# Expert weights loaded as 2 MiB units in 16 KB pieces, gate before up, with all gathers ahead of gate's second half

## The reference

```
x <- LN1(alpha * x + (sum_b sigmoid(G_b) * (mixer_b @ w_branch[b])) @ w_out)
# hierarchical MoE: softmax over 4 groups, best group; top 2 of its 4 experts
h   = silu(x @ w_gate[e]) * (x @ w_up[e])        # [tokens, 512] per expert, 16 experts
ffn = sum_e combine[t, e] * (h[e] @ w_down[e])   # [tokens, 2048]
x <- LN2(alpha * x + ffn)
```

## Time and profile before

| | |
|---|---|
| median of the runs | 1325.91 us |
| the profiled execution's own time | 1324.61 us |
| its span in the profile | 1322.9 us |
| PE busy | 1308.2 us |
| DMA moved | 364.97 MB, mean 276 GB/s |
| TensorE's granted clock | full speed |

### The profile page before, as it was taken

How to read it: one execution, slowest core, us unless ns; L and a number is a source line. 1 busy time by engine, 2 the same in 40 slices (tenths; PEclk the granted TensorE clock), 3 DMA queues, 4 the chain that set the end, 5 groups by cost and what they waited for, 6 DMA issues and landing times.

```text
span 1322.9 us, 17951 instructions
## 1 busy us (share of the span) xinstructions
PE 1308.2 (99%) x7379; PEld 959.7 (73%) x7379; DVE 569.2 (43%) x741; ACT 476.6 (36%) x667; POOL 29.5 (2%) x55
## 2 busy tenths in 40 slices
PE   9999999999999999999999999999999999999998
PEld 9999989998888888888888888844453444544443
DVE  4367445356555644464455555525112121221206
ACT  4535343346556544454333433422121121211212
POOL 1000000400000000000100001000000000000000
PEclk9999999999999999999999999999999999999999
DMA  9965555544454445554556795699999999999996
GB/s 302 344 230 197 175 190 188 190 160 160 159 161 156 160 154 194 174 174 159 191 190 226 262 393 178 264 416 416 422 420 422 420 421 421 421 421 420 422 408 253
DMA packets 122100, 364.97 MB, mean 276 GB/s; under 512 B 11627, under 2 KB 19243, under 8 KB 98486
## 3 DMA queue, kind: packets, MB, share of 16 engines
q1 hardware_dynamic: 115430, 359.06, 73.1%
q10 hardware_dynamic: 6608, 5.02, 1.3%
HBM read 361.96 MB, written 2.10 MB: 275 GB/s over the span
## 4 chain that ended last, share of the span: by engine, by line
PE 93%; DMA 3%; DVE 2%; ACT 0%; issue 0%; SPq 0%; DVEq 0%; ACTq 0%
PE main L1212 19%; PE main L1214 19%; PE main L1213 19%; PE main L556 16%; PE att L646 7%; PE att L510 5%; DMA mraw<-in_expert_w_down_dram 3%; PE att L1453 1%; PE main L522 1%; PE main L523 1%; PE att L1436 1%; PE att L1472 1%; PE att L1468 1%; DVE wlo L1866 1%; PE att L1423 0%; PE att L617 0%
## 5 line engine op out<-in xcount | busy, mean ns | idle before, releaser
L1866 DVE TENSOR_TENSOR wlo<-raw,whi 128x2048 fp32r<-128x2048 f32 x135 | 310.3, 2299 | 360.3 <-ACT whi L1619 360.3
L1619 ACT ACTIVATE whi<-raw 128x2048 fp32r<-128x2048 f32 x135 | 258.1, 1912 | 420.4 <-PE main L1214 418.9
L556 PE MATMUL main<-mraw,xg 128*64 128x512 f32 x1024 | 225.4, 595 | 1.5 <-DMA mraw<-in_expert_w_up_dram 1.4
L1212 PE MATMUL main<-whi,xhi 128*128 128x512 f32 (+1 forms) x544 | 203.9, 375 | 0.0
L1214 PE MATMUL main<-whi,xlo 128*128 128x512 f32 (+1 forms) x544 | 201.7, 371 | 0.0
L1213 PE MATMUL main<-wlo,xhi 128*128 128x512 f32 (+1 forms) x544 | 201.6, 371 | 0.0
L556 PEld LDWEIGHTS main<-mraw,xg 128*64 128x64 f32 x1024 | 72.1, 137 | 137.4 <-issue 136.2
L1212 PE MATMUL main<-xhi,whi 128*128 128x256 f32 (+1 forms) x560 | 159.6, 285 | 1.1 <-DVE wlo L1997 1.0
L1213 PE MATMUL main<-xlo,whi 128*128 128x256 f32 (+1 forms) x560 | 158.4, 283 | 0.0
L1214 PE MATMUL main<-xhi,wlo 128*128 128x256 f32 (+1 forms) x560 | 158.4, 283 | 0.0
L1214 PEld LDWEIGHTS main<-whi,xlo 128*128 128x128 f32 x544 | 102.5, 188 | 17.7
(11 more groups left out here) (336 smaller groups left out, 1300.8 us busy)
## 6 DMA issues: line engine op xcount, KB each, us to landing
raw<-in_w_in_dram SPq DMA_DIRECT2D x95, 1024.0 KB, 5.1
mraw<-in_expert_w_gate_dram SPq DMA_DIRECT2D x64, 1024.0 KB, 21.3
mraw<-in_expert_w_up_dram SPq DMA_DIRECT2D x64, 1024.0 KB, 22.4
mraw<-in_expert_w_down_dram SPq DMA_DIRECT2D x58, 1024.0 KB, 23.1
raw<-in_w_branch_dram SPq DMA_DIRECT2D x24, 1024.0 KB, 5.0
raw<-in_w_out_dram SPq DMA_DIRECT2D x16, 1024.0 KB, 7.9
mraw<-in_expert_w_down_dram SPq DMA_DIRECT2D x12, 512.0 KB, 9.3
xin<-in_x_dram SPq DMA_DIRECT2D x4, 512.0 KB, 8.2
```

The lines of the kernel that those rows point to most:

```text
L556: ins = pe.matmul(main[0][half, w, :], xg[:, k, half], src[:, kk * DE:(kk + 1) * DE], start=(k == 0), stop=(k == KT - 1))
L1212: pe.matmul(o, ah, bh, start=start, stop=False, skip_group_check=skip)
L1619: act.activation(whi[:, u % SPLIT, 0:n], raw[:, slot, 0:n], ACT.Copy).then_inc(hi_done, 1)
L1866: dve.tensor_tensor(wlo[:, u % SPLIT, 0:n], raw[:, slot, 0:n], whi[:, u % SPLIT, 0:n].bitcast(F32), ALU.subtract).then_inc(lo_done, 1)
```

## The change

The unit of a weight load doubles: 1024 rows of gate or up, or 256 rows of down, of one expert, as 128 partitions x 16 KB, each one contiguous read. A pair now has MU = 12 units in the order gate rows 0-1023 (experts 0, 1), gate rows 1024-2047, up the same, then down. PE runs `products(w, h)`: gate's first half, then gathers 2 and 3 and the transposes, then gate's second half, then all of up. Row blocks within 1024 rows are now interleaved (a partition holds 8 consecutive rows), so the tokens are written in a matching order to a new tile `xn` by 8 activations of 512 columns instead of 2 of 2048, and gather q waits only for its own two (`z_ok`). LN1's scale and shift are needed in the new order too: `gbx` is loaded and transposed in the w_out stage besides `gb`. The first 10 units (20 MiB) have places as before. The ring behind them has 8 places of 2 MiB instead of 19 of 1 MiB: `khT`/`qst` are not used as places, and `xlo` and `qbT`/`sig` hold one unit once each. A place is free when PE has used its whole 2 MiB. Six early units (5, 6, 8, 9, 10, 11) are loaded as two 1 MiB halves. The last pair's down keeps its column quarters. `out_acc` moves from `O2` to `xlo`.

The lines of the diff that matter (lines that only rename or index tiles are left out):

```
-MRAW = 19
+RING = 8
 Z = 5
 STEPS = 2 * GROUP
-MU = 24
+MU = 12
+GU = 8
...
+        xn, out_acc = at("xn", O2, [P, T, D]), at("out_acc", made["xlo"], [P, T, D])
...
-        once = range(len(places), len(places) + 3)
-        places += [O2, O2 + 8192, made["qbT"]]
+        places += [made["xlo"], made["xlo"] + 8192, made["qbT"]]
...
+        raw_at = {(places[j] - made["raw"]) // 8192: j for j in range(6, 6 + RAW)}
+        w_at = [(12, 17), (13, 18)] if places[12] < places[17] else [(17, 12), (18, 13)]
+        ring = [(0, 1), (2, 3), (4, 5), *((raw_at[n], raw_at[n + 1]) for n in range(0, RAW, 2)), *w_at]
+        first = [*ring[:7], (14, 15), ring[7], (16, 19)]
+        assert len(ring) == RING and all(places[a] + 8192 == places[b] for a, b in ring + first[:9])
+        NF = len(first)
+        IN_HALVES = (5, 6, 8, 9, NF, NF + 1)
+        doubles = {a: at(f"mtwo{a}", places[a], [P, 2 * UNIT]) for a, _ in ring + first[:9]}
...
         def place(g):
-            if g < NP:
-                return g
-            return second_round[g - NP] if g < GROWN else ring[(g - GROWN) % MRAW]
+            return first[g] if g < NF else ring[(g - NF) % RING]
 
         def user_before(g):
-            return max((e for e in range(g) if place(e) == place(g)), default=None)
-
-        LOOP0, LAST0 = (FIRST * MU - GROWN) % MRAW, (FIRST * MU + MU - GROWN) % MRAW
-        L2R = MU - MRAW
-        l2g, l2b, ysb = (at(n, places[ring[(LAST0 + L2R + j) % MRAW]], [P, D]) for j, n in enumerate(("l2g", "l2b", "ysb")))
+            return max(e for e in range(g) if place(e) == place(g))
...
+            if r < GU:
+                h, name = r % 4 // 2, ("expert_w_gate", "expert_w_up")[r // 4]
+                rows = A[name][0, bass.ds(e, 1), h * 1024:(h + 1) * 1024, :]
                 return rows.rearrange("a (p k) f -> p a (k f)", p=P)
-            if quarters:
-                c = (r - 4 * QUADS) // 2
-                return A["expert_w_down"][0, bass.ds(e, 1), :, c * 512:(c + 1) * 512].rearrange("a (f p) n -> p (a f) n", p=P)
-            kf = (r - 4 * QUADS) // 2
-            return A["expert_w_down"][0, bass.ds(e, 1), kf * P:(kf + 1) * P, :].rearrange("a p d -> p a d")
+            j = (r - GU) // 2
+            return A["expert_w_down"][0, bass.ds(e, 1), j * 256:(j + 1) * 256, :].rearrange("a (p i) d -> p a (i d)", p=P)
...
         def moe_loads(sp):
-            first_units(sp, range(6, NP))
-            for w in range(2):
-                for g in (NP + 2 * w, NP + 2 * w + 1):
-                    sp.wait_ge(lt_out, g - NP + 2)
-                    load_half(sp, g, 0)
-                for g in (NP + 2 * w, NP + 2 * w + 1):
-                    sp.wait_ge(m_used, user_before(g) + 1)
-                    load_half(sp, g, 1)
-            for g in range(NP + 4, FIRST * MU):
-                if user_before(g) is None:
-                    sp.wait_ge(acc_ok, 1)
-                else:
-                    sp.wait_ge(m_used, user_before(g) + 1)
+            sp.wait_ge(lo_done, U1 + 11)
+            load_half(sp, 5, 1)
+            for g in (3, 4):
+                sp.wait_ge(lo_done, U1 + 7 + 2 * g)
+                load_unit(sp, g, 0, place(g))
+            sp.wait_ge(lo_done, U1 + 16)
+            load_half(sp, 5, 0)
+            late = (U1 + 15) % SPLIT
+            sp.wait_ge(unit_used, U1 + 15)
+            load_half(sp, 6, 1 - late)
+            load_half(sp, 8, 1 - late)
+            sp.wait_ge(unit_used, U1 + 16)
+            load_half(sp, 6, late)
+            load_half(sp, 8, late)
+            load_half(sp, 9, 0)
+            sp.wait_ge(r_ps, T)
+            load_half(sp, 9, 1)
+            sp.wait_ge(z_ok, 2 * QUADS)
+            load_unit(sp, 7, 0, place(7))
+            sp.wait_ge(lt_out, 3)
+            for g in (NF, NF + 1):
+                load_half(sp, g, 0)
+            for g in (NF, NF + 1):
+                sp.wait_ge(m_used, user_before(g) + 1)
+                load_half(sp, g, 1)
+            for g in range(NF + 2, FIRST * MU):
+                sp.wait_ge(m_used, user_before(g) + 1)
                 load_unit(sp, g % MU, g // MU, place(g))
...
-                    sp.wait_ge(m_used, m * MU + FIRST * MU + r - MRAW + 1)
-                    load_unit(sp, r, (m + FIRST) % PAIRS, ring[(LOOP0 + r) % MRAW])
-            for r in range(MU):
-                sp.wait_ge(m_used, turns * MU + FIRST * MU + r - MRAW + 1)
-                if r < MU - 2:
-                    load_unit(sp, r, PAIRS - 1, ring[(LAST0 + r) % MRAW], quarters=True)
-                else:
-                    load_last(sp, r, 0, mlanded[ring[(LAST0 + r) % MRAW]])
-            for r in range(MU - 2, MU):
-                load_last(sp, r, 1, wr_in)
+                    sp.wait_ge(m_used, m * MU + FIRST * MU + r - RING + 1)
+                    load_unit(sp, r, (m + FIRST) % PAIRS, ring[(LOOP0 + r) % RING])
+            for r in range(GU):
+                sp.wait_ge(m_used, turns * MU + FIRST * MU + r - RING + 1)
+                load_unit(sp, r, PAIRS - 1, ring[(LAST0 + r) % RING])
+            for c in range(4):
+                for a in range(2):
+                    if c % 2 == 0:
+                        sp.wait_ge(m_used, turns * MU + FIRST * MU + GU + c + a - RING + 1)
+                    load_quarter(sp, c, a, slice(0, 512 if c < 3 else 256), mlanded[quarter_place(c, a)])
+            for a in range(2):
+                load_quarter(sp, 3, a, slice(256, 512), wr_in)
...
+                pe.wait_ge(z_ok, 2 * q + 2)
...
+                def products(w, h):
+
+                    for kk in range(8):
+                        k = 8 * h + kk
+                        if kk % 4 == 0:
+                            if w == 0:
+                                pe.wait_ge(xg_out, 1 + k // 4 + m * 4)
+                            for a in range(2):
+                                arrived(4 * w + 2 * h + a, kk // 4)
                         for a in range(2):
+                            src = tile(4 * w + 2 * h + a, kk // 4)
+                            half = slice(a * SLOTS, (a + 1) * SLOTS)
+                            ins = pe.matmul(main[0][half, w, :], xg[:, k, half], src[:, kk % 4 * DE:(kk % 4 + 1) * DE],
+                                            start=(k == 0), stop=(k == KT - 1))
+                            if kk == 7:
+                                ins.then_inc(m_used, 1)
+                            elif kk == 3 and fixed == 0 and h == 0 and w == 0:
+                                ins.then_inc(lt_out, 1)
...
                 put(1)
                 gather(1)
                 put(2)
-                gate_up(0)
+                products(0, 0)
                 gather(2)
-                gate_up(1)
                 if fixed != 0:
                     pe.wait_ge(y_lo, m * 4)
                 gather(3)
                     ins = pe.matmul(main[1][:, 1, S:S + 2], cmb[:, t, :], ones[:, 0:2], start=(t == 0), stop=(t == 1),
                                     skip_group_check=True)
                 ins.then_inc(ws_t, 1)
-                gate_up(2)
-                gate_up(3)
+                products(0, 1)
+                products(1, 0)
+                products(1, 1)
                 put(3)
                 for j in range(2):
                     pe.wait_ge(h_ok, 1 + j + m * 2)
...
-            for t in range(T):
-                act.activation(xr[:, t, :], xr[:, t, :], ACT.Identity, bias=nmr[:, t:t + 1],
-                               scale=rstd[:, t:t + 1]).then_inc(z_ok, 1)
+            for q in range(4):
+                half = slice(q // 2 * 1024, (q // 2 + 1) * 1024)
+                for t in range(T):
+                    src = xr[:, t, half].rearrange("p (c k m b) -> p b k c m", c=2, k=4, b=2)[:, q % 2]
+                    act.activation(xn[:, t, q * 512:(q + 1) * 512].rearrange("p (k c m) -> p k c m", k=4, c=2), src, ACT.Identity,
+                                   bias=nmr[:, t:t + 1], scale=rstd[:, t:t + 1]).then_inc(z_ok, 1)
...
-                act.wait_ge(m_used, 4 * QUADS + m * MU)
+                act.wait_ge(m_used, GU // 2 + m * MU)
...
+                dve.wait_ge(m_used, GU + m * MU)
...
-                dve.wait_ge(m_used, once[1] + 1)
+                dve.wait_ge(m_used, GU)
...
+                    if u == U1 + 6:
+                        sp.wait_ge(m_ps, 8)
+                        for j, name in enumerate(("ln1_g", "ln1_b")):
+                            sp.dma_start(gbx[2 * j:2 * j + 2, :], A[name][0].rearrange("(h n) -> h n", h=2)).then_inc(gbx_in, 16)
                     if u in (U1 + 7, U1 + 9, U1 + 11):
-                        first_units(sp, range(u - U1 - 7, u - U1 - 5))
+                        g = (u - U1 - 7) // 2
+                        sp.wait_ge(unit_used, U1)
+                        if g == 2:
+                            sp.wait_ge(gb_ps, 2)
+                        load_unit(sp, g, 0, place(g))
                     src = A["w_out"][0, q * 512:(q + 1) * 512, c * 512:(c + 1) * 512]
```

(42 more changed lines are left out.)

126 lines of the change are left out of this document (48 added, 78 removed).

## The result

The changed kernel takes 1337.45 us (median of 4 runs, 1336.99 to 1338.21) against 1325.8 for the kernel before: a ratio of 1.0089, interval 1.0071 to 1.0106, or 11.8 us slower. The prediction said 1335.2 us in a range from 1329 to 1341: slower, by 2.3 us less than measured. The profiled execution took 1337.57 us, its span is 1335.8 us, the granted clock 0.996 of full speed.

The account below looks back on a forecast made before the run. The weight stream was taken to bound the MoE and set the end. The terms, 0.9 + 2.4 + 0 + 9.5 - 5.4 + 1.9 = +9.3 us, gave 1335.2 us on the median, in a range from 1329 to 1341.

Parts of the forecast that it names:

- gbx transposes: In the w_out stage after unit U1+8: eight added transposes on PE's chain cost 0.9 us, bounds 0.57 and twice 0.57.
- wait for `gb_ps` 2: In the w_out stage: SP waits for the second transposes before issuing U1+11, stalling PE 2.4 us, bounds 0.4 to 6.0.
- start of the MoE: Eight short activations replace two, silu of gate runs under up's products: together zero, 0.4 gained to 0.7 lost.
- ring: In pairs 0 and 1: places come free later, the weight stream falls 3.8 MiB behind, 9.5 us, bounds zero and 12.
- pieces of 16 KB: Weight stream after 44 MiB: a fixed 9.7 ns per piece is saved, 5.4 us gained, bounds nothing and 11.3.
- last pair: Up's last products need 4 MiB, then take 7.02 us; PE, not the last load, ends it, 1.9 us later.
- What bounds the kernel: The MoE is a stream of weights at 416 to 421 GB/s; PE's own work is a floor 5.2 us below.
- The wait ahead of U1+11: The w_out stage's wait for `gb_ps` 2: U1+11 issued at 810.9, PE able to start it at 825.4, not 823.0.
- A stall of 2.4 us: Before U1+11 in the w_out stage: PE's predicted idle time, taken as the whole cost of the wait.
- The saving on silu: In pair 0: silu of gate runs under up's products, saving ACT's 0.4 us.
- the smaller ring: The prediction's heading for the ring term of 9.5 us in pairs 0 and 1, called the largest term.
- Both upper rivals: Stream rate with bigger pieces: 435 GB/s, 1329.3 us, chance 0.10; above 440 GB/s, all losses made up, chance 0.03.

Follow-up runs that it names:

- e1: Changed kernel, but expert unit 2 and its wait for the second transposes issued behind w_out unit U1+15; 1331.72 us.
- e12: e6 with two normalising activations of 2048 columns in plain order, the column reordering left out; 1327.98 us.
- e2: Changed kernel, but each 2 MiB load issued as two DMAs of 128 x 8 KB, same place, order and release; 1341.62 us.
- e5: Changed kernel, but in pairs 0 and 1 the 2 MiB refill loads issued as halves, each behind half a unit's use; 1334.63 us.
- e6: Changed kernel with the edits of e1 and e5 together; 1329.64 us.
- e3: Kernel before, with a ring of 16 instead of 19 places of 1 MiB; 1326.42 us.
- e4: Kernel before, with all of gate before up and gathers moved as in the change, 1 MiB units and 19 places kept; 1327.18 us.
- e7: Kernel before, with the edits of e4 and e3 together: gate-first order and 16 places of 1 MiB, released one by one; 1327.03 us.
- e9: e7 with SP's waits for a place rounded up to groups of four units (4 MiB), units still 1 MiB; 1330.21 us.
- e10: e9, and PE also waits for all four units of a group (4 MiB) before beginning the first; 1331.98 us.

## Why the prediction was right, point by point

| term | predicted | measured | from |
|---|---|---|---|
| gbx transposes | +0.9 | +0.98 | chain; e1 |
| wait for `gb_ps` 2 | +2.4 | +4.65 | 5.63 - 0.98; e1 says 5.4 |
| start of the MoE, to the first product | 0 | +0.8 | 6.42 - 5.63; e12 |
| ring | +9.5 | +8.3 | 15.7 - 0.96 - 6.42 |
| pieces of 16 KB | -5.4 | -5.0 | 303 us (950 to 1252.85) x 7 / 428; e2 says -4.2 |
| last pair | +1.9 | +1.2 | 11.94 - 10.76 |
| sum | +9.3 | +10.9 | whole: 12.9 - 0.96 = 11.94 |

The 1.0 us between the sum and the whole is within the rounding of the rates: half a GB/s is 0.36 us over 303 us and 0.25 us over the two windows of 210 us, in each kernel.

- **What bounds the kernel** was right: the stream, from the start of the MoE on. A loss ahead of it (e1) and a loss inside it (e5) both came back at the end nearly whole, and they added (e6), as far as steps of 2 to 3 us tell.
- **The wait ahead of U1+11** was right in each link, and its gap well sized: 2.8 us for 2.4. The step that was mis-sized is "A stall of 2.4 us" as the whole cost. PE came back at the lower clock, 1.7 us more by the 8.5 slow steps. The other 0.2 us has no place. The term came to 4.65 us, within its bounds of 0.4 to 6.0. This alone is 2.3 us, most of the 2.6 between forecast and result.
- **The start of the MoE** was to cost nothing, between 0.4 gained and 0.7 lost; it cost 0.8. The row used, one activation of 512 columns with 0.60 us, was a plain copy. These, with a scale and a bias per partition, take 0.76. That makes them 2.0 us longer than the two long ones, and 0.85 of it shows as PE's wait for `xg`; the rest fell into time in which PE was still at its gathers. Also wrong was that the finer `z_ok` brings nothing: PE's gathers ran from 866.31 to 870.15, and the last of the eight activations ended at 867.86. A wait for all eight would have held the gathers 1.5 us, to 871.7, and the first product would have started there and not at 871.01: 0.7 us more, an estimate. The saving on silu came as forecast, behind the first product: PE's wait for `hh` in pair 0 is 0.67 us, where it was 1.09. With it the term is near 0.4.
- **The ring** had the right size, 8.3 for 9.5, since the count of MiB that SP may have issued at PE's release times was right. But the name "the smaller ring" was wrong. Fewer places cost 1.1 us (e3), the order 1.7 (e4), both together also 1.7 (e7). Release by 4 MiB, two units at once, costs 3.4 more (e9) and arrival by 4 MiB 1.3 more (e10). These make 6.5 of the loss. The working had this in it ("only then are units 2 and 3 given free"): it counted the grain and the place together, and no term told them apart. What the grain of 4 MiB costs with 16 places already in pair 1, no run shows by itself; the windows of e1 and e9 put it 2.9 us above e9.
- **The pieces** were right: 428 GB/s for a predicted 427 to 428. The Trainium skill's 3 cycles a packet (DMA: Bandwidth & Descriptors, Why small descriptors are slow) would have given 2.0 us, an estimate; the trace's rates give 5.0, and e2 gives 4.2 with some 3 us of uncertainty. So it is the rates, and the packets' 12 ns in e2, that decide for the rows' 9.7 ns a piece. Both upper rivals fall: no 435, let alone 440 GB/s.
- **The last pair** was right in that PE, not the last quarter, now ends it. But the chain doesn't pass up's last units at all; it leaves the stream at pair 6's down. The mechanism of the term, that PE must have 4 MiB and then has twice the work left, is at work there: 7.09 instead of 3.65 us behind the last landing, 3.4 more. The lower clock adds 1.7 (8.78 instead of 7.09). Against them stand the waits for weights that the kernel before still had behind this point, 1.4 us for up and 1.4 for the quarters, of which 0.3 is left, and about 1.4 us of a shorter path on PE that wasn't taken apart. What remains is the 1.2 us. The size was near by luck: the place was wrong, and the clock wasn't in the sum.

**What stays open.** Added up by experiments the changed kernel is 5.4 (stall) + 1.0 (gbx) + 0.8 (xn) + 6.5 (e10) - 4.2 (pieces) = 9.5 us over before, where 11.8 were measured. The 2.3 us are of the size of the summed intervals. The traces point to a place for them: the 2.9 us by which the changed kernel's stream falls behind e9's in pair 1, since e9 and e10 may issue one MiB of its down 12 us sooner. No run has 16 places in pair 1 and units of 1 MiB, so this isn't tested. A kernel with 16 KB pieces whose units are released in steps of 1 MiB in all pairs wasn't tried. No version that was run beats the kernel before.

## What to carry to other kernels

When a double-size transfer unit is weighed, count three things apart: the rate it gains over the whole stream, what its coarser release loses once, in the first rounds of the ring, where the queue runs dry, and what its coarser arrival loses where the consumer has caught up. Here 5 us gained stood against some 8. When an experiment imitates a ring, count its first round too: here a place more in that round was enough to hide part of the loss. A wait put into an in-order issue queue for a single load holds every load behind it; look for a later place for it before anything else, since e1's few lines gave back 5.4 us. And a gap in TensorE's work of near 3 us can cost more than its length.

## What the hardware showed beyond expectation

- After waits of 2.7 to 2.9 us TensorE's granted clock was at the lower level for several us: 0.53 from 826.75 to 830.35, steps of 0.43 instead of 0.23 us, and 8.78 instead of 7.09 us for 32 matmul records at 1133.86 and 1252.85 (granted clock 0.61 from 1252.85 to 1256.50). Not each wait of this length did it: at 1194.10 the wait was 2.68 us and the 32 took 7.09, at 1252.85 it was 2.69 and they took 8.78. Why the one was spared stays open.

```profile
1194.10 2.37 PE L673 MATMUL att<-mtwo,hT 128*64 128x512 f32 x10 [2.68 <-DMA mtwo<-in_expert_w_down_dram]
...
1252.85 2.10 PE L673 MATMUL att<-mtwo,hT 128*64 128x512 f32 x6 [2.69 <-DMA mtwo<-in_expert_w_down_dram]
```

  In the kernel before, with no wait for weights above 1.4 us, the clock was 1.00 throughout.
- Activations of 512 columns with scale and bias per partition took 0.76 us each back to back (0.72 contiguous), so eight take 6.07 us for the columns that two of 2048 did in 4.08.
- One core moved 428 GB/s for 300 us in 16 KB pieces and 421 in 8 KB pieces, in the same kernel with nothing else changed but that each DMA was split in two (e2).
